# Three fused transformer blocks on one core: third mixer rescheduled, both gated merges started with the attention branch

## The chip, the cores and the metric

One NeuronCore of a Trainium2 chip runs the whole program. The metric is device time in microseconds (us) of one execution. PE is TensorE, ACT ScalarE, DVE VectorE, POOL GpSimd and SP SyncE; SP issues nearly all loads.

## What is computed

Three blocks run one after the other on x of 512 tokens by 1024 channels: a conformer/sparse attention block with MLPs, a block with an RWKV-7 branch and a sliding-window attention branch, and a block with a stick-breaking attention branch and a state-space (S5) branch. The change touches the mixers of the second and third block and the feed-forward between them:

```
# block 2, mixer                      (y_rwkv, y_att: 512 x 512)
merged = sigmoid(g_rwkv) * (y_rwkv @ w_branch_rwkv) + sigmoid(g_att) * (y_att @ w_branch_attn)
x = x + merged @ w_out
x = x + 0.5 * (silu(h @ w_gate) * (h @ w_up)) @ w_down ; x = rms_norm(x)
# block 3, mixer
q, k, v, u, g_sb, g_ssm = split(h @ w_in)
z = q k^T / 8 ; log_beta = log_sigmoid(z) ; log_one_minus = where(causal, log_beta - z, 0)
after = reverse_cumsum(log_one_minus) - log_one_minus
y_sb = (where(causal, exp(log_beta + after), 0) @ v) @ w_sb_up            # 8 heads of 64
state = powers * state + B u ; y = Re(C state) + D u                      # 32 groups, 64 states, complex
y = gelu(y) ; y = y * sigmoid(y @ w_glu + b_glu) ; y_ssm = y @ w_ssm_up
x = layer_norm(alpha * x + (1 + g_m) * ((sigmoid(g_sb) * y_sb + sigmoid(g_ssm) * y_ssm) @ w_out))
```

## The kernel before

**Split products.** Activations lie transposed (channels on partitions, 512 tokens along the free axis). Each large product is made of three TensorE passes over numbers split in a high and a low part: `hi*ah + hi*al + lo*ah` (`lin`). A weight slab of 128x2048 numbers is loaded by SP into one of three buffers `raw`, split by GpSimd into `whi` and `wlo` (lines 143 and 136, three slots each), and used by TensorE in 48 matmuls of 128x512. ACT writes the high part of an activation (`ah`, `hh`, `yh`) and DVE subtracts it for the low part (`al`, `hl`, `yl`).

**Order.** Nothing is scheduled at run time: each engine runs its own program, in the order in which the methods `*_pe`, `*_act`, `*_dve` are written, and semaphore counts say what it waits for. SP's loads follow the order in which TensorE's program asks for slabs. PSUM is a ring of six banks for `lin`; a bank is taken in program order and waits until its last reader has given it back. All small operations are recorded at helper lines (113 and 116 matmul and transpose, 131 ACT, 136 to 167 DVE).

**Second mixer.** `rwkv_order` runs the recurrence in chunks; the tiles of the recurrence lie in the memory of `whi` and `wlo`, so the first slab behind it is split only when TensorE, ACT and DVE have ended it. Then come eight high parts and eight low parts of the two branches (`yh`, `yl`), and `merge_pe`: for each half of the columns the RWKV branch, then the attention branch, 48 matmuls each. `merge_dve` multiplies the first branch's banks with gates read back from DRAM (`gr <- bank, sq`), adds the second branch, and splits the result.

**Feed-forward before the third block.** `mlp_dve` handles groups of four hidden tiles in two turns; behind each turn the call `turns(g)` lets DVE do some steps of the preparation of the state-space tables (`ssm_setup_dve`: powers L, input matrices b, angle tables T, decay rho; mostly 128x16 operations on `macc`). Behind the second turn of a group DVE must add the down-projection's eight banks to x.

**Third mixer.** `mixer3_pe` first runs eight slabs for the gates. Behind slabs 2, 4, 6 and 8 `tables_pe(j)` makes the table set j of four: 16 transposes (XT, from XB) and 16 small products (KS, from XB and WC). DVE makes XB and WC of the next set when KS of the last is done on TensorE and WC has been written to DRAM by ACT's DMA. Then come six slabs of features and two for v, and the **stick**: `stick_steps` runs 20-odd steps in which the stages of the stick-breaking attention are staggered. A stage is given a lag: step s runs `scores` of unit pair s, `sums` of s-1, `after` of s-2 and `values` of s-3. Between them, every four steps, a quarter j of the state-space branch is worked off: at step 4j+1 its inputs (`in`, bank<-U,raw), on DVE the rotation, a scan along time and the states H; at 4j+2 and 4j+3 the outputs (`y`, from U and H), and at 4j+4 the turn back. U, four shifted copies of the features u, is gathered by 16 DMAs on SP's queue (`load_u`), behind the end of the input stage. After the stick come GELU, the `glu` product and the merge as in the second block.

## Time and profile before

| | |
|---|---|
| median of 3 runs | 3972.09 us (3970.39 to 3974.9) |
| the profiled execution | 3981.96 us, its span 3980.2 us |
| TensorE busy | 3533.6 us (89%) |
| VectorE busy | 1944.2 us (49%) |
| GpSimd busy | 1623.0 us (41%) |
| ScalarE busy | 754.4 us (19%) |
| mean granted TensorE clock | 0.926 |

The profiled execution is 9.9 us (0.25%) longer than the median. A number in brackets at the end of a timeline row is how long the engine had been idle ahead of it and what ended that. Sections are found by time: the second mixer's merge is at 2399 to 2483 us, the second feed-forward at 2531 to 2932, the gates and tables of the third mixer at 2967 to 3112, the stick at 3203 to 3382, the glu product and the merge at 3393 to 3483.

### The profile page before, as it was taken

The numbers are of one execution on the slowest core, as the hardware profiler recorded it, in microseconds if no ns is written. First come the engines' busy times: TensorE is split into PE (matmuls) and PEld (weight loads), VectorE is DVE, ScalarE is ACT, GpSimd is POOL, SyncE is SP. The second block draws the span as 40 slices with busy tenths as digits, with TensorE's granted clock in tenths as the row PEclk, the third lists the DMA queues.
The fourth block names the chain that finished last, engine by engine and source line by source line (L and its number), as shares of the span: only waits on it lengthen the run. The fifth ranks groups of instructions, "written<-read, shape, count | busy, mean of one in ns | idle before, by whom it ended". The sixth has DMA issues, their size and how long they took to land. (4 is left out here: it accounts for less than half of the span.)

```text
span 3980.2 us, 44783 instructions
## 1 busy us (share of the span) xinstructions
PE 3533.6 (89%) x18996; PEld 2730.4 (69%) x18996; DVE 1944.2 (49%) x2919; ACT 754.4 (19%) x1638; POOL 1623.0 (41%) x486
## 2 busy tenths in 40 slices
PE   7989999679999999999997876999978977789998
PEld 5757888556578887788785675787746744548885
DVE  2244455337844546534245556556585235544234
ACT  2241011224521011001105221100021133121001
POOL 4404556140045666556540004565533400525552
PEclk9999999678999999999996788999989977899999
DMA  4202333220023434323420003222225232312220
GB/s 141 69 22 90 121 128 106 67 98 1 1 74 105 139 106 127 117 95 96 127 85 10 2 2 117 80 95 96 85 85 174 83 106 95 116 53 85 96 95 32
DMA packets 250679, 340.45 MB, mean 86 GB/s; under 512 B 9808, under 2 KB 180048, under 8 KB 247920
## 3 DMA queue, kind: packets, MB, share of 16 engines
q1 hardware_dynamic: 227600, 300.43, 23.1%
q10 hardware_dynamic: 22880, 37.16, 2.8%
q8 instruction: 150, 2.46, 0.2%
q14 instruction: 49, 0.40, 0.0%
HBM read 307.95 MB, written 25.43 MB: 84 GB/s over the span
## 5 line engine op out<-in xcount | busy, mean ns | idle before, releaser
L143 POOL TENSOR_SCALAR whi<-raw 128x2048 fp32r<-128x2048 f32 x241 | 487.3, 2022 | 2276.9 <-PE bank L113 1307.4
L136 POOL TENSOR_TENSOR wlo<-raw,whi 128x2048 fp32r<-128x2048 f32 x241 | 1137.2, 4718 | 20.1
L113 PE MATMUL bank<-ah,whi 128*128 128x512 f32 x2392 | 958.4, 401 | 64.3 <-DVE al L146 40.3
L113 PE MATMUL bank<-al,whi 128*128 128x512 f32 x2392 | 952.3, 398 | 0.0
L113 PE MATMUL bank<-ah,wlo 128*128 128x512 f32 x2392 | 951.0, 398 | 0.0
L113 PEld LDWEIGHTS bank<-ah,whi 128*128 128x128 f32 x2392 | 452.8, 189 | 188.2 <-issue 38.5
L113 PEld LDWEIGHTS bank<-ah,wlo 128*128 128x128 f32 x2392 | 453.1, 189 | 111.7
L113 PEld LDWEIGHTS bank<-al,whi 128*128 128x128 f32 x2392 | 453.2, 189 | 110.4 <-issue 1.2
L113 PE MATMUL bank<-hh,whi 128*128 128x512 f32 x1040 | 414.2, 398 | 14.5 <-DVE x L146 14.5
L113 PE MATMUL bank<-hl,whi 128*128 128x512 f32 x1040 | 412.9, 397 | 0.0
L113 PE MATMUL bank<-hh,wlo 128*128 128x512 f32 x1040 | 412.9, 397 | 0.0
L113 PEld LDWEIGHTS bank<-hh,whi 128*128 128x128 f32 x1040 | 196.5, 189 | 63.5 <-DVE x L146 15.8
L113 PEld LDWEIGHTS bank<-hh,wlo 128*128 128x128 f32 x1040 | 196.2, 189 | 48.2
L113 PEld LDWEIGHTS bank<-hl,whi 128*128 128x128 f32 x1040 | 196.5, 189 | 47.7
L136 DVE TENSOR_TENSOR scr<-gt,bank 128x512 f32<-128x512 f32 x66 | 45.2, 686 | 343.8 <-PE bank L113 343.2
L136 DVE TENSOR_TENSOR hl<-scr,hh 128x512 fp32r<-128x512 f32 x66 | 200.3, 3072 | 0.2
L136 DVE TENSOR_TENSOR x<-x,bank 128x512 f32<-128x512 f32 x128 | 86.0, 685 | 162.1 <-PE bank L113 162.1
L146 DVE SCALAR_TENSOR_TENSOR x<-bank,x 128x512 f32<-128x512 f32 x120 | 80.0, 687 | 165.8 <-PE bank L113 165.8
L131 ACT ACTIVATE gt<-gt 128x512 f32<-128x512 f32 x108 | 68.2, 634 | 394.1 <-DVE gt L136 391.2
L131 ACT ACTIVATE hh<-gt 128x512 fp32r<-128x512 f32 x64 | 40.0, 625 | 535.9 <-DVE gt L146 535.9
L136 DVE TENSOR_TENSOR hl<-gt,hh 128x512 fp32r<-128x512 f32 x64 | 126.5, 1998 | 28.0 <-ACT gt L131 28.0
L146 DVE SCALAR_TENSOR_TENSOR gt<-bank,rb 128x512 f32<-128x512 f32 x64 | 44.1, 691 | 147.5 <-PE bank L113 147.3
(388 smaller groups left out, 4320.9 us busy)
## 6 DMA issues: line engine op xcount, KB each, us to landing
raw<-in_w_in SPq DMA_DIRECT2D x34, 1024.0 KB, 5.3
raw<-in_w_mlp_in SPq DMA_DIRECT2D x32, 1024.0 KB, 5.5
raw<-in_w_mlp_out SPq DMA_DIRECT2D x32, 1024.0 KB, 6.6
raw<-in_w_ada SPq DMA_DIRECT2D x24, 1024.0 KB, 5.2
raw<-in_ffn_w_gate SPq DMA_DIRECT2D x22, 1024.0 KB, 5.3
raw<-in_ffn_w_up SPq DMA_DIRECT2D x22, 1024.0 KB, 5.3
raw<-in_ffn_w_down SPq DMA_DIRECT2D x22, 1024.0 KB, 5.0
raw<-in_w_ffn_in SPq DMA_DIRECT2D x22, 1024.0 KB, 5.0
```

The lines of the kernel that those rows point to most:

```text
L113: return self.eng.matmul(out, lhsT, rhs, start=start, stop=stop, skip_group_check=True)
L131: return self.eng.activation(out, src, func, scale=scale, **kw)
L136: return IDLE if self.eng is None else self.eng.tensor_tensor(out, a, b, op)
L143: return self.eng.tensor_scalar(out, a, s1, s2, op0, op1)
L146: return IDLE if self.eng is None else self.eng.scalar_tensor_tensor(out, a, s, b, op0, op1)
```

## The change

Five things, in the order of the program. (1) Both merges begin with the attention branch; its high and low parts are made during the recurrence (in the second mixer beside `scan(2)`, in the third in steps 16 to 18 of the stick). (2) `ssm_setup_dve` is cut at the input matrices: 8 steps a turn in place of 20 (and 15 in place of 18 in the first part), and the angle tables (`ssm_turns_dve`) are made behind the last table set. (3) `tables_pe` is divided: XT stays where it was, KS comes one slab later. (4) The first gather of U goes into the tile yM, which is not lent from the weight buffers, and no longer waits for the end of the input stage. `values` runs at lag 4, the scan and H one step after the rotation, y at lags 3 and 4, the turn at lag 6. (5) In the third mixer the first merge block stands ahead of glu. Its slab may be split when the last `after` product and the third quarter's outputs are done, and glu's slab when `lw` of the last unit and the last quarter's outputs are done.

```diff
+    def ended(self, name):
+
+        return lambda: [x.at("end", name) for x in (self.P, self.C, self.D)]
...
-                    self.some(first, 18)
+                    self.some(first, 15)
                 elif g > 2:
-                    self.some(second, 20)
+                    self.some(second, 8)
...
-        self.merge_pe(e, "mrg2", self.mrg2, (A["w_branch_rwkv_2"][0], A["w_branch_attn_2"][0]), "rwkv")
+        self.merge_pe(e, "mrg2", self.mrg2, (A["w_branch_rwkv_2"][0], A["w_branch_attn_2"][0]),
+                      lambda i: self.ended("rwkv"))
...
+    def high_of_branch_act(self, a, name, T, br, src, tiles=range(4)):
+        for k in tiles:
+            a.f(T["hi"][br][:, k, :], src[:, k, :], ACT.Copy).then_inc(*self.C.up(name, "hi part", br, k))
+
+    def low_of_branch_dve(self, d, name, T, br, src, tiles=range(4)):
+        for k in tiles:
+            d.wait_ge(*self.C.at(name, "hi part", br, k))
+            d.tt(T["lo"][br][:, k, :], src[:, k, :], T["hi"][br][:, k, :].bitcast(F), SUB).then_inc(
+                *self.D.up(name, "lo part", br, k))
+
+    @staticmethod
+    def merge_order(T):
+
+        return [(half, br) for half in range(2) for br in (T["first"], 1 - T["first"])]
+
+    def merge_pe(self, e, name, T, Ws, after, between=None):
+
+        for i, (half, br) in enumerate(self.merge_order(T)):
+            self.lin(e, (name, half, br), Ws[br], 0, 4, [512 * half + 128 * n for n in range(4)],
+                     lambda k, br=br: (T["hi"][br][:, k, :], T["lo"][br][:, k, :]),
+                     lambda k, br=br: self.D.at(name, "lo part", br, k), after=after(i))
+            if i == 0 and between:
+                between()
...
+        self.U4 = [t["yM"], far["U1"], far["U0"], far["U1"]]
...
-                 between=lambda n: self.tables_pe(e, n // 4) if n % 4 == 2 else None)
+        def tables(n):
+            if n % 4 == 2:
+                self.tables_in_pe(e, n // 4)
+            elif n:
+                self.tables_own_pe(e, n // 4 - 1)
+        self.lin(e, "gates3", W, 0, 8, [2048 + 128 * n for n in range(16)], self.xact, normed, between=tables)
         self.lin(e, "feat", W, 0, 8, [128 * n for n in range(8)] + [1536 + 128 * n for n in range(4)], self.xact,
-                 normed)
+                 normed, between=lambda n: None if n else self.tables_own_pe(e, 3))
...
+        assert Clock.draft or self.n_split % 3 == self.MERGE_SLOT, self.n_split
+        first = lambda: [P.at("st", "a", 31), P.at("ssm", 2, "y", 1)]
+        second = lambda: [D.at("st", "lw", 31), P.at("ssm", 3, "y", 1)]
+
+        def glu():
+            self.lin(e, "glu", A["w_glu_3"][0], 0, 4, [128 * n for n in range(4)],
+                     lambda k: (self.ah[:, 4 + k, :], self.al[:, 4 + k, :]), lambda k: D.at("glu", "lo", k), after=second)
+        self.merge_pe(e, "mrg3", self.mrg3, (A["w_sb_up_3"][0], A["w_ssm_up_3"][0]),
+                      lambda i: self.ended("stick") if i else first, glu)
...
+        def tables(n):
+            if n and n % 4 == 0:
+                self.tables_in_act(a, n // 4 - 1)
+            elif n > 4 and n % 4 == 2:
+                self.tables_own_act(a, n // 4 - 1)
+        self.gates_act(a, "gates3", self.gates3, tables)
+        self.tables_in_act(a, 3)
+        self.tables_own_act(a, 3)
...
+        d.wait_ge(*C.at("nmix3", "hi", 7))
+        self.ssm_turns_dve(d)
...
-        self.stick_steps((3, values), (2, after), (0, scores), (None, lambda s: self.ssm_pe(e, s)))
+        self.stick_steps((4, values), (2, after), (0, scores), (None, lambda s: self.ssm_pe(e, s)))
...
+        def early(s):
+
+            if 16 <= s < 19:
+                a.wait_ge(*P.at("st", "s", 31))
+                a.wait_ge(*C.now())
+                self.high_of_branch_act(a, "mrg3", self.mrg3, 0, m["yS"], [s - 16])
+        self.stick_steps((None, lambda s: self.ssm_act(a, s)), (4, values), (2, after), (0, scores), (None, early))
...
-        self.stick_steps((3, values), (2, after), (1, sums), (None, lambda s: self.ssm_dve(d, s)))
+        def early(s):
+            if 16 <= s < 19:
+                self.low_of_branch_dve(d, "mrg3", self.mrg3, 0, self.m3["yS"], [s - 16])
+        self.stick_steps((3, values), (2, after), (1, sums), (None, lambda s: self.ssm_dve(d, s)), (None, early))
...
+    def ssm_turns_dve(self, d):
+
+        D, m, tmp = self.D, self.m3, self.scr.tiles[2]
+        T, rho, t16 = [m["T0"], m["T1"]], m["rho"], tmp[:, 0:16]
+        co, si, m8, er, ei, e2r, e2i = (self.small[:, i, :] for i in (4, 5, 7, 12, 13, 14, 15))
+        d.wait_ge(*D.now())
+        self.cmul_dve(d, (er, ei), (co, si), (co, si), t16)
+        d.wait_ge(*D.now())
+        run(self.turns_of_angles(d, T, rho, tmp, t16, m8, er, ei, e2r, e2i))
...
-        e.wait_ge(*self.P.at("end", "mix3 in"))
-        if j > 1:
-            e.wait_ge(*self.P.at("ssm", j - 2, "y", 1))
+        if j:
+            e.wait_ge(*self.P.at("end", "mix3 in"))
+        else:
+            e.wait_ge(*self.P.at("tables", 3, "KS", 1))
+            e.wait_ge(*self.tab_out["WC"].at(3))
+        if j == 3:
+            e.wait_ge(*self.P.at("ssm", 1, "y", 1))
...
-        j = self.ssm_piece(s, 4)
+        j = self.ssm_piece(s, 6)
...
-            j = self.ssm_piece(s, 2 + q2)
+            j = self.ssm_piece(s, 3 + q2)
...
+        j = self.ssm_piece(s, 2)
+        if j is not None:
+            js = slice(4 * j, 4 * j + 4)
+            rh = m["rho"][:, js, :].rearrange("p q m -> p (q m)")
+            last()
+            d.scan(hr, rh, gr, 0.0, MUL, ADD).then_inc(*D.up())
+            d.scan(hi, rh, gi, 0.0, MUL, ADD).then_inc(*D.up())
+            last()
+            if j:
...
+    def other_branch(self):
+
+        self.a.wait_ge(*self.D.at("wkv", 1, "ARBK"))
+        for k in range(4):
+            yield
+            self.net.high_of_branch_act(self.a, "mrg2", self.net.mrg2, 1, self.net.m2["yA"], [k])
```

TensorE at the first table set, before: the last two transposes of XB, KS (WC with XB), and the next gate slab (ah, al with whi). "waits" names the engines whose semaphores are awaited.

```order
L116 MATMUL bank<-cst,XB_186_115 128x128
L116 MATMUL bank<-cst,XB_187_116 128x128
L113 MATMUL bank<-WC_188_117,XB_186_115 32x256 [waits dve,act]
L113 MATMUL bank<-WC_189_118,XB_187_116 32x256
...
L113 MATMUL bank<-WC_188_117,XB_186_115 32x256
L113 MATMUL bank<-WC_189_118,XB_187_116 32x256
L113 MATMUL bank<-ah,whi_6 128x512 [waits pool,act]
L113 MATMUL bank<-al,whi_6 128x512
```

The same KS products after the change: they stand behind the slab in whi_6, and ahead of that in whi_4.

```order
L113 MATMUL bank<-al,whi_6 128x512
L113 MATMUL bank<-ah,wlo_9 128x512
L113 MATMUL bank<-WC_190_119,XB_188_117 32x256 [waits dve,act]
L113 MATMUL bank<-WC_191_120,XB_189_118 32x256
...
L113 MATMUL bank<-WC_190_119,XB_188_117 32x256
L113 MATMUL bank<-WC_191_120,XB_189_118 32x256
L113 MATMUL bank<-ah,whi_4 128x512 [waits pool,act]
L113 MATMUL bank<-al,whi_4 128x512
```

48 matmuls have come between the transposes and KS.

SP at the end of the third mixer's input loads, as a piece of the difference: the 16 DMAs of the first gather (U or yM from u).

```order
 L106 DMA raw_2<-in_w_in 128x4x512 [waits pool]
-L106 DMA U_222_151<-u_102 32x512 [waits tab_WC,act,tab_TM,pe,tab_XT,pool]
-L106 DMA U_222_151<-u_102 32x512 x3
-L106 DMA U_222_151<-u_102 32x511 x4
-L106 DMA U_222_151<-u_102 32x510 x4
-L106 DMA U_222_151<-u_102 32x509 x4
+L106 DMA yM_105<-u_104 32x512 [waits tab_WC,act,tab_TM,pe,tab_XT,pool]
+L106 DMA yM_105<-u_104 32x512 x3
+L106 DMA yM_105<-u_104 32x511 x4
+L106 DMA yM_105<-u_104 32x510 x4
+L106 DMA yM_105<-u_104 32x509 x4
 L106 DMA raw_3<-tables 128x2048
```

The place in the queue is the same; the destination is another, and the count of TensorE's semaphore behind "pe" is now that of the last KS product.

VectorE in the first quarter of the stick, before: scan (scr from rho), the products that give the states H, and then the logarithms `lw` of the step behind.

```order
L167 SCALAR_TENSOR_TENSOR scr_18<-rho_113,scr_17 128x256 [waits dve]
L167 SCALAR_TENSOR_TENSOR scr_18<-rho_113,scr_17 128x256
L136 TENSOR_TENSOR H_224_153<-scr_18,T_182_111 128x4x64 [waits dve]
L136 TENSOR_TENSOR rb<-scr_18,T_183_112 128x256
L136 TENSOR_TENSOR H_224_153<-H_224_153,rb 128x4x64 [waits dve]
L136 TENSOR_TENSOR H_225_154<-scr_18,T_183_112 128x4x64
L136 TENSOR_TENSOR rb<-scr_18,T_182_111 128x256 [waits dve]
L136 TENSOR_TENSOR H_225_154<-H_225_154,rb 128x4x64 [waits dve]
L136 TENSOR_TENSOR lw_214_143<-lw_214_143,bank 128x128 [waits pe,dve]
L136 TENSOR_TENSOR lw_215_144<-lw_215_144,bank 128x128 [waits pe]
```

After: rotation, then the step's logarithms, and only a step later scan and H.

```order
L136 TENSOR_TENSOR rb<-bank,T_185_114 128x256 [waits dve]
L136 TENSOR_TENSOR scr_17<-scr_17,rb 128x256 [waits dve]
L136 TENSOR_TENSOR lw_208_137<-lw_208_137,bank 128x128 [waits pe]
...
L167 SCALAR_TENSOR_TENSOR scr_18<-rho_115,scr_17 128x256 [waits dve]
L167 SCALAR_TENSOR_TENSOR scr_18<-rho_115,scr_17 128x256
L136 TENSOR_TENSOR H_226_155<-scr_18,T_184_113 128x4x64 [waits dve]
L136 TENSOR_TENSOR rb<-scr_18,T_185_114 128x256
L136 TENSOR_TENSOR H_226_155<-H_226_155,rb 128x4x64 [waits dve]
L136 TENSOR_TENSOR H_227_156<-scr_18,T_185_114 128x4x64
L136 TENSOR_TENSOR rb<-scr_18,T_184_113 128x256 [waits dve]
L136 TENSOR_TENSOR H_227_156<-H_227_156,rb 128x4x64 [waits dve]
```

Between the rotation and the scan 12 instructions of the attention now stand (the first is shown, 11 are left out at the dots).

## Rows read from the trace of the kernel before

**Rows 1.** The page, costliest groups: busy us, mean ns | idle before, releaser.
```profile
L113 PE MATMUL bank<-ah,whi 128*128 128x512 f32 x2392 | 958.4, 401 | 64.3 <-DVE al L146 40.3
```

**Rows 2.** Waits of PE, whole span: total us, times, longest us.
```profile
PE bank L113 <- DVE lw L136: 38.6, 8, 7.0
...
PE bank L113 <- DVE WC L136: 23.6, 4, 9.5
...
PE bank L113 <- DMA raw<-tables: 13.9, 1, 13.9
...
PE bank L113 <- DVE H L136: 3.9, 1, 3.9
```

**Rows 3.** Timeline, second mixer's merge: start us, us, instruction [idle before <-releaser].
```profile
2401.41 14.14 DVE L136 TENSOR_TENSOR yl<-yR,yh 128x512 fp32r<-128x512 f32 x4 [0.76 <-ACT yh L131]
...
2407.76 0.79 PE L113 MATMUL bank<-yh,whi 128*128 128x512 f32 x1 [8.55 <-POOL wlo L136]
...
2431.36 0.77 PE L113 MATMUL bank<-yh,whi 128*128 128x512 f32 x1 [10.17 <-DVE gr L136]
```

**Rows 4.** Timeline, second feed-forward: VectorE and TensorE.
```profile
2656.60 1.39 DVE L136 TENSOR_TENSOR gt<-bank,rb 128x512 f32<-128x512 f32 x2 [9.81 <-PE bank L113]
...
2723.80 1.39 DVE L136 TENSOR_TENSOR gt<-bank,rb 128x512 f32<-128x512 f32 x2 [9.81 <-PE bank L113]
...
2771.64 4.68 DVE L136 TENSOR_TENSOR b<-b,tmp 128x256 f32<-128x256 f32 x1
...
2798.05 1.39 DVE L136 TENSOR_TENSOR gt<-bank,rb 128x512 f32<-128x512 f32 x2 [9.81 <-PE bank L113]
...
2873.26 1.39 DVE L136 TENSOR_TENSOR gt<-bank,rb 128x512 f32<-128x512 f32 x2 [9.81 <-PE bank L113]
...
2905.87 0.51 PE L113 MATMUL bank<-hh,whi 128*128 128x512 f32 x1 [3.94 <-DVE x L146]
```

**Rows 5.** Timeline, third mixer's gates and tables.
```profile
2995.10 3.61 PE L113 MATMUL bank<-WC,XB 128*32 128x256 f32 x16 [1.41 <-DVE WC L136]
...
3032.53 5.68 PE L113 MATMUL bank<-WC,XB 128*32 128x256 f32 x16 [9.47 <-DVE WC L136]
...
3038.62 1.56 ACTq L106 DMA_DIRECT2D tables<-WC  x2
...
3045.56 1.29 DVE L136 TENSOR_TENSOR g<-L,b 128x512 f32<-128x512 f32 x2 [13.18 <-DMA tables<-WC]
...
3052.69 5.72 DVE L136 TENSOR_TENSOR g<-L,sp 128x576 f32<-128x576 f32 x2
```

**Rows 6.** Windows: PE, PEld, DVE, ACT, POOL busy, PEclk; one period of the stick.
```profile
3298.00:3338.70 40.70, 29.82 (x133) 18.16 (x133) 22.13 (x65) 14.84 (x35) 0.00 (x0) 0.79 0.32 103
```

**Rows 7.** TensorE by shape in 3298.0 to 3338.7: busy us, mean ns | idle.
```profile
L113 PE MATMUL bank<-U,raw 128*128 128x64 f32 x33 | 4.4, 302 | 0.0
L113 PE MATMUL bank<-raw,U 128*64 128x256 f32 x16 | 4.3, 393 | 0.0
L113 PE MATMUL bank<-raw,H 128*64 128x256 f32 x16 | 4.1, 379 | 0.0
L113 PE MATMUL bank<-mb,cst 128*128 128x512 f32 x4 | 3.8, 1047 | 0.0
```

**Rows 8.** Timeline, the stick: TensorE and VectorE.
```profile
3255.20 1.02 PE L113 MATMUL bank<-mb,cst 128*128 128x512 f32 x2
...
3301.90 0.42 DVE L136 TENSOR_TENSOR scr<-bank,T 128x256 f32<-128x256 f32 x1 [2.43 <-PE bank L113]
...
3308.86 1.97 PE L113 MATMUL bank<-lw,v 128*64 128x512 f32 x4 [7.00 <-DVE lw L136]
```

**Rows 9.** Timeline, after the stick: GpSimd and TensorE.
```profile
3388.23 4.81 POOL L136 TENSOR_TENSOR wlo<-raw,whi 128x2048 fp32r<-128x2048 f32 x1
...
3393.14 0.77 PE L113 MATMUL bank<-yh,whi 128*128 128x512 f32 x1 [11.18 <-POOL wlo L136]
...
3421.25 0.77 PE L113 MATMUL bank<-yh,whi 128*128 128x512 f32 x1 [14.22 <-DVE yl L136]
```

More of the change, by code:

```diff
@@ L330, in gpsimd @@
             raw, hi, lo = self.raw[slot], self.whi[j % self.NSPL], self.wlo[j % self.NSPL]
-            if after:
-                for other in (self.P, self.C, self.D):
-                    g.wait_ge(*other.at("end", after))
+            for w in after() if after else ():
+                g.wait_ge(*w)
             g.wait_ge(*self.raw_in[slot].at(i))
@@ L1899, in merge_act @@
         for i, (half, br, n) in enumerate(order):
+            if i == 4 and between:
+                between()
             if i + 1 < 16:
                 bring(i + 1)
-            if br:
+            if br != T["first"]:
                 m = 4 * half + n
@@ new lines, in merge_dve @@
+        for half, br in self.merge_order(T):
+            if i == 4 and between:
+                between()
+            for n in range(4):
+                m, key, second = 4 * half + n, ((name, half, br), n), br != T["first"]
+                g = self.sq.of(name, half, br, n)
+                if second:
+                    s, free = self.scr.take(name, m)
+                    d.wait_ge(*free)
+                d.wait_ge(*self.P.at(*key))
+                d.wait_ge(*self.gate_in[i % 2].at(name, half, br, n))
+                i += 1
+                dst = s[:, :] if second else T["gr"][:, n, :]
+                d.tt(dst, self.ps.of(*key)[:, :], g[:, :], MUL).then_inc(*self.ps.give(D, *key))
+                self.sq.also(D, name, half, br, n)
+                if second:
+                    d.wait_ge(*D.now())
+                    d.tt(s[:, :], s[:, :], T["gr"][:, n, :], ADD).then_inc(*D.up(name, "value", m))
+                    d.wait_ge(*self.C.at(name, "hi", m))
+                    d.tt(self.al[:, m, :], s[:, :], self.ah[:, m, :].bitcast(F), SUB).then_inc(
+                        *self.scr.give(D, name, m))
@@ L1940, in rwkv_order @@
         run(together(e.inverse(1, 0), e.inverse(1, 1), e.parts(1)))
-        run(e.scan(2))
+        run(together(e.scan(2), e.other_branch()))
         run(together(e.scan(3), e.post(2)))
@@ L2076, in mixer3_pe @@
         self.barrier(e, P, "stick", True)
-        T = self.mrg3
-        self.lin(e, "glu", A["w_glu_3"][0], 0, 4, [128 * n for n in range(4)],
-                 lambda k: (T["yh"][:, k, :], T["yl"][:, k, :]), lambda k: D.at("glu", "yl", k), after="stick")
-        self.merge_pe(e, "mrg3", T, (A["w_sb_up_3"][0], A["w_ssm_up_3"][0]))
+        assert Clock.draft or self.n_split % 3 == self.MERGE_SLOT, self.n_split
[6 more added lines that the diff above has]
+                      lambda i: self.ended("stick") if i else first, glu)
         self.lin(e, "out3", A["w_out_3"][0], 0, 8, [128 * n for n in range(8)], self.xact,
@@ L2502, in tables_act, with tables_own_act @@
                 ACT.Copy).then_inc(*self.ps.give(C, "tables", j, "XT", q))
+        a.wait_ge(*C.at("tables", j, "XT", 3))
+        a.dma(self.tables[j, 0], t["XT"][:, :, :, :, :].rearrange("p q b r n -> p (q b r n)")).then_inc(
+            *out["XT"].up(j))
+    def tables_own_act(self, a, j):
+        P, C, D, t, out = self.P, self.C, self.D, self.tab_t, self.tab_out
         if j:
@@ L2511, in tables_act @@
                 *self.ps.give(C, "tables", j, "KS", q2))
-        a.wait_ge(*C.at("tables", j, "XT", 3))
-        a.dma(self.tables[j, 0], t["XT"][:, :, :, :, :].rearrange("p q b r n -> p (q b r n)")).then_inc(
-            *out["XT"].up(j))
         for ri in range(2):
@@ new lines, in ssm_dve @@
+        j = self.ssm_piece(s, 2)
+        if j is not None:
+            js = slice(4 * j, 4 * j + 4)
+            rh = m["rho"][:, js, :].rearrange("p q m -> p (q m)")
+            last()
+            d.scan(hr, rh, gr, 0.0, MUL, ADD).then_inc(*D.up())
+            d.scan(hi, rh, gi, 0.0, MUL, ADD).then_inc(*D.up())
+            last()
+            if j:
+                d.wait_ge(*P.at("ssm", j - 1, "y", 1))
+            q3 = lambda ap: ap.rearrange("p (q m) -> p q m", q=4)
+            self.cmul_dve(d, [x[:, :, 1:65] for x in self.H], [q3(hr), q3(hi)], [x[:, js, :] for x in T], q3(w))
+            D.mark("ssm", j, "H")
@@ L3232, in post, with other_branch @@
         d.tt(m["yR"][:, :, at], m["yR"][:, :, at], t4, ADD).then_inc(*net.scr.give(D, "wkv", "t", p))
+    def other_branch(self):
+        for k in range(4):
+            yield
+            self.net.low_of_branch_dve(self.d, "mrg2", self.net.mrg2, 1, self.net.m2["yA"], [k])
 def _constants():
```

195 lines of the change are left out of this document (74 added, 121 removed).

## Prediction

> **What bounds the kernel now.** I read the page's busy shares first: TensorE 89%, VectorE 49%, GpSimd 41%. Nine tenths of TensorE's time are products with a weight slab [rows 1], which the change leaves as they are: 48 matmuls, 11.2 us a slab (a feed-forward group of six slabs takes 67.20 us, below). So time can only come from TensorE's waits and from its slow stretches. Second, the list of its waits over the span [rows 2]: `lw` of VectorE 38.6 us in 8 waits, `WC` 23.6 in 4, a table load 13.9 in one, `H` 3.9 in one. All four lie in the third mixer. Third, the timelines around them and around the two merges [rows 3, 5, 8, 9], and the second feed-forward [rows 4], where a wait shows at one place only although three groups are stretched. Last the window table of one period of the stick [rows 6]: in 40.70 us TensorE is busy 29.82 and its granted clock is 0.79. Neither engine fills the period; they wait for each other in turn.
>
> All sums are made against the profiled execution, 3981.96 us, 9.9 above the median.
>
> **Second mixer's merge: -11 us.** The first wait, 8.55 us, is for GpSimd's split of a slab that may begin only behind the recurrence [rows 3]; the change leaves that condition, so it stays. The second is 10.17 us for the gate product `gr` [rows 3]. It is late because VectorE first makes eight `yl`, four in 14.14 us, so 3.5 each. The attention's four now move beside the recurrence. The other four end at 2401.4 + 14.1 = 2415.5. The first branch's four banks come from one slab, side by side, at about 2407.8 + 11.2 + 1 = 2420, and are multiplied then; TensorE, which ran out of banks at 2431.4 - 10.2 = 2421.2, waits under 1: -9.5. Behind the wait the first matmul takes 0.77 us where the mean is 401 ns [rows 1, 3]; without the pause this slow restart goes: -2. The moved instructions are four copies and four `yl`; they land in a place where VectorE is short, and cost 0 to 3 us, I take 0.7 (free of GpSimd a 128x512 product of VectorE takes 1.39 / 2 = 0.7 [rows 4]). Range 7 to 12.5.
>
> On the 3.5 us: in the timeline a `yl` takes five times as long while GpSimd splits [rows 3]. The Trainium skill ("SBUF — State Buffer", Who interferes with whom) says that a VectorE instruction with two SBUF inputs and a GpSimd one that reads SBUF exclude each other for whole instructions; by that rule, the trace agrees.
>
> **Second feed-forward: -19 us.** The multiplication `gt` marks the same point in each group, always after an idle of 9.81 us [rows 4]. From 2656.60 to 2723.80 a group takes 67.20 us, which is the bare six slabs; the next two take 74.25 and 75.21. They lose 7.05 and 8.01, and a third one at the end has its wait in the list, 3.94 [rows 4], with about 1.5 of slow restart. Together 20.6. The cause is the 20 table steps a turn: VectorE comes late to the bank additions. One 128x256 step caught by a GpSimd split takes 4.68 [rows 4]. With 8 steps a turn the additions start in time, unless such a step is caught again; for that I take off 1.5. The angle tables that were made here go behind the last table set, where TensorE has eight slabs of features and v (8 x 11.2 = 90 us) that ask nothing of them. They are some 90 instructions, most on 128x16; even at 0.7 each that is 63: 0, and if GpSimd stretches them past the 90, the stick starts late by the excess. Range 12 to 21.
>
> **Gates and tables: -11 us.** Now TensorE waits for `WC` at every KS (one 9.47 [rows 5]), 23.6 in all, and three of the four KS run slow, 5.68 where the first takes 3.61 [rows 5]: 3 x 2.1 and some 1.3 on the slabs behind, 7.6. With one slab (11.2) between XT and KS both go: -31. But VectorE may begin the next XB only when KS of the last set is done and `WC` is stored. That chain now starts 11.2 us later and only one slab is left ahead of the next XT. From the DMA's issue to VectorE's restart the trace has 3038.62 to 3045.56, 7 us; XB itself takes 3045.56 to 3052.69, 7.1 [rows 5], and 4 us more when GpSimd catches it. 14.1 to 18.4 against 11.2: XT waits 3 to 7, once more than that since the first `WC` store was slower; I take 5, three times, 15, and 5 for slow restarts. -31 + 20 = -11. Range 2 to 18.
>
> **The stick: -54 us.** It lasts 179 us now (3203 to 3382). What goes: the table load 13.9, which queues on SP behind 16 gather DMAs that wait for the end of the input stage; `H` 3.9; `lw` 38.6, since a quarter's rotation, scan and H now stand in two steps. 56.4 in all [rows 2]. One of these `lw` waits is 7.00, and VectorE's run of the quarter begins at 3301.90, 6.3 us before its first logarithm [rows 8].
> What comes: `y` now waits for H, which VectorE makes one step behind the rotation. VectorE's way from `in` to H is 6.3 (the quarter's own work) + 0.75 (yM) + the attention's share of a step, (22.1 - 7.05)/4 = 3.8 [rows 6]: 10.9. TensorE has two steps of attention between, (29.8 - 3.5 - 12.8)/4 = 3.4 each, where 3.5 is slow clock (next sentence) and 12.8 the state-space products [rows 6, 7], + 0.7: 7.5. So 3.4 a period, about 13 over four. The clock: four `mb` products take 3.8 us, 1047 ns each [rows 7], two take 1.02 at the upper level [rows 8]; that is 1.8 lost on them, I estimate as much on their neighbours, 3.5 a period, 14 in all. With shorter waits I count 11 of it back. -56.4 + 13 - 11 = -54. A period becomes about 29 us; its floor is TensorE's 26.3 (29.8 - 3.5), above VectorE's 22.1 [rows 6]. The gather into yM has its 16 DMAs earlier in SP's queue behind the same loads; the three later gathers have whole periods. Range 40 to 60.
>
> **After the stick: -8.5 us.** Now TensorE waits 11.18 for a slab whose split can begin only when all is done (`wlo` alone 4.81) and 14.22 for `yl` [rows 9]. The first merge block's slab is split some 3 us before the stick ends: the split takes between 4.81 and 11.18 us, I take 6.7, and the wait becomes about 3.5. Behind that block, glu needs four low parts of GELU at 3.5 each under GpSimd's lock, 14, against its 11.2 us: a new wait of about 4.4. The 14.22 falls to about 9, as its first branch's parts are done and `gr` is needed later, but `yl` of the second still follows glu. 7.7 - 4.4 + 5.2 = 8.5. Range 2 to 14. The split meets VectorE's last `lw` steps; one caught instruction there costs up to 4.8.
>
> **Sum.** -11 - 19 - 11 - 54 - 8.5 = -103.5: 3878.5 in a profile like the one shown, 3869 on the median's level.
>
> **Rivals.**
> *A, the tables' wait only moves.* XT comes late by what KS was late: with the chain at 18.4 twice and at 22 once the waits are 7.2, 7.2 and 11, 11 more than the 15 taken. For it: VectorE idles 13.18 for the store [rows 5], so the chain, not VectorE, is the limit. Against: two of three XB runs are short. The gates gain 0: 3880.
> *B, the stick becomes bound by VectorE's latency.* Each of its instructions for a step waits for TensorE and the reverse, and 22.1 busy us come with idle before each. The period stays 35: 4 x 6 more than forecast, 3893. For it: VectorE waits 2.43 for a bank even at the rotation [rows 8]. Against: the two-step distance gives each side a spare step.
> *C, the gather isn't earlier.* It stands at the same place on SP's queue, behind waits for slabs; if the slab loads ahead set its time, the 13.9 stay: 3883.
> *D, slower: TensorE stays at its lower clock through the stick.* The rows show both levels there: 1047 ns and 510 ns for the same `mb` product, which is 1.2 against 2.4 GHz [rows 7, 8]. If the denser row of small products with short waits were granted the lower level throughout, its 26.3 a period double to 52.6, 4 x 52.6 + 10 = 220 against 179 now: +41, less the 50 gained elsewhere. It decides once this reaches the slabs: a merge block at the lower level costs 11.2 more, so from one block on the kernel is slower, and with all five of merge and glu +47, 4019. Against: waits shrink, and in the page's row all slabs average 401 ns, the upper level.
> [...]
>
> **How the numbers follow.** Forecast 0.66, A 0.12, B 0.15, C 0.03, D 0.04. The likeliest gives 3869; its own terms, taken apart, reach from 3850 to 3890, and B to 3893; with gaps added up the range is 3850 to 3905. A measurement of this kernel tells 0.2% (8 us) from no change. Every case but D lies 60 us or more below; of D half is within 0.2% and half slower: faster 0.96, same 0.02, slower 0.02.
>
> **What would show it.** Merge 2: no wait by `gr` over 2 us, the 8.5 before it still there. Feed-forward: all `gt` distances 67.2. Gates: no wait by `WC`, KS at 3.6, three waits by XB of 3 to 10. Stick: no wait by the table load, `lw` under 5 in all, waits by `H` about 13, period near 29, clock above 0.9. Tail: TensorE back within 4 us, a wait by `al` of about 4 before glu. Wrong if the stick's period stays above 33, if the clock there falls, or if the angle tables delay the first step.

## The result

| | before | changed |
|---|---|---|
| median | 3972.77 us (3970.39 to 3974.9, 4 runs) | 3847.99 us (3846.75 to 3848.68, 4 runs) |
| ratio | | 0.9686, 95% interval 0.9669 to 0.9703 |
| profiled execution, span | 3980.2 us | 3846.9 us |
| TensorE busy, mean granted clock | 3533.6 us, 0.926 | 3495.2 us, 0.942 |

124.8 us faster (3.1%). The forecast was 3869 us with a range of 3850 to 3905: the direction and four fifths of the size are right, and the time is 2 us below the range. The two profiles differ by 133.3 us, more than the medians, since the profiled execution before was a long one. By stretches that is as follows. A stretch goes from the first product of one part on TensorE to the first product of the next; only the stick is counted to the end of its last product, where the row of glu and the merge begins.

| stretch, us | before | changed | difference | forecast |
|---|---|---|---|---|
| up to the second mixer's merge | 2407.8 | 2402.2 | -5.6 | 0 |
| second merge, up to the feed-forward | 123.6 | 109.2 | -14.4 | -11 |
| second feed-forward | 401.6 | 380.5 | -21.1 | -19 |
| norms between | 34.2 | 34.2 | 0 | 0 |
| gates, tables, features, v | 235.7 | 205.4 | -30.3 | -11 |
| stick | 179.1 | 129.2 | -49.9 | -54 |
| glu and third merge | 101.1 | 87.5 | -13.6 | -8.5 |
| rest | 497.1 | 498.8 | +1.7 | 0 |

The first row can't be put down to the change. The changed kernel and its eleven variants below, alike up to that point, reach the merge between 2394.2 and 2407.5 us, and the kernel before reached it at 2407.8 and, in the last experiment, at 2400.5. Most of this comes from one stretch of the recurrence and from what lies ahead of it; the last section has the numbers. A few microseconds between the medians of two kernels say little here; a later stretch that an edit leaves alone repeats within 1 or 2 us (2.5 for the second merge). So the experiments are read by stretches first.

### The profile page after: what moved, and what is told of

Its sections match the earlier page's. It is cut to its first block, busy times and chain, and to the rows that moved or that the text cites. A ratio compares the mean times of both kernels' runs of the same rounds, so it can differ in the third digit from the quotient of the medians.

```text
span 3846.9 us, 44799 instructions
## 1 busy us (share of the span) xinstructions
PE 3495.2 (91%) x18996; PEld 2710.7 (70%) x18996; DVE 1898.0 (49%) x2919; ACT 751.9 (20%) x1638; POOL 1620.0 (42%) x486
## 4 chain that ended last, share of the span: by engine, by line
PE 84%; DVE 10%; ACT 3%; issue 1%; DMA 1%; POOL 1%; ACTq 0%; DVEq 0%; SPq 0%; POOLq 0%
PE bank L113 81%; PE bank L116 3%; DVE scr L136 1%; DVE al L146 1%; DVE rb L136 1%; DVE rb L158 1%; DVE x L146 1%; DVE st L151 0%; ACT ah L131 0%; ACT L131 0%; DMA raw<-in_ffn_w_gate 0%; POOL wlo L136 0%; ACTq L106 0%; ACT p L131 0%; DMA macc<-in_masks 0%
## 5 line engine op out<-in xcount | busy, mean ns | idle before, releaser
L146 DVE SCALAR_TENSOR_TENSOR gt<-bank,rb 128x512 f32<-128x512 f32 x64 | 44.1, 691 | 146.7 <-PE bank L113 146.5
```

Source lines behind the costliest of these rows:

```text
L146: return IDLE if self.eng is None else self.eng.scalar_tensor_tensor(out, a, s, b, op0, op1)
```

## The profile after

TensorE's waits in the changed kernel (us in total, times, longest). In [rows 2] stood `lw` 38.6, `WC` 23.6, table load 13.9, `H` 3.9.

```profile
PE bank L113 <- DVE lv L136: 8.7, 4, 7.9
...
PE bank L113 <- DVE yl L136: 8.1, 1, 8.1
...
PE bank L113 <- DVE gr L136: 5.4, 2, 2.7
...
PE bank L113 <- DVE H L136: 4.9, 3, 2.2
...
PE bank L113 <- ACT yM L131: 4.9, 1, 4.9
```

`WC` and the table load are gone, and no `XB` has come. For `lw` (half of it is called `lv` now) TensorE waits once for long, at the stick's end. One wait is new and stood in no forecast: `rs` of VectorE, 8.0 us in four waits of the stick, the longest 3.8.

```profile
PE bank L113 <- DVE rs L155: 8.0, 4, 3.8
```

Timeline of the second merge and of `gt` in the feed-forward:

```profile
2402.15 0.79 PE L113 MATMUL bank<-yh,whi 128*128 128x512 f32 x1 [8.54 <-POOL wlo L136]
...
2427.76 0.47 PE L113 MATMUL bank<-yh,whi 128*128 128x512 f32 x1 [1.60 <-DVE scr L136]
```

```profile
2636.36 1.39 DVE L136 TENSOR_TENSOR gt<-bank,rb 128x512 f32<-128x512 f32 x2 [9.81 <-PE bank L113]
...
2703.56 1.39 DVE L136 TENSOR_TENSOR gt<-bank,rb 128x512 f32<-128x512 f32 x2 [9.81 <-PE bank L113]
...
2770.76 1.39 DVE L136 TENSOR_TENSOR gt<-bank,rb 128x512 f32<-128x512 f32 x2 [9.81 <-PE bank L113]
...
2837.96 1.39 DVE L136 TENSOR_TENSOR gt<-bank,rb 128x512 f32<-128x512 f32 x2 [9.81 <-PE bank L113]
```

The wait of 10.17 [rows 3] is gone, the 8.5 ahead of it has stayed, and all three distances of `gt` are 67.20, where two were longer [rows 4]. Both steps did what the prediction wrote, with one exception: a second, shorter wait by `gr` stands in the merge, 2.72 us in the kernel before and 2.72 now, and the prediction had said that none over 2 us would be left.

The tables, by engine (TensorE, ScalarE's queue, VectorE, GpSimd); these answer to [rows 5]:

```profile
2950.71 1.91 PE L116 MATMUL bank<-cst,XB 128*128 128x128 f32 x16
2963.75 3.64 PE L113 MATMUL bank<-WC,XB 128*32 128x256 f32 x16
2978.62 1.91 PE L116 MATMUL bank<-cst,XB 128*128 128x128 f32 x16
```

```profile
2954.39 0.33 ACTq L106 DMA_DIRECT2D tables<-XT  x1
...
2967.43 0.94 ACTq L106 DMA_DIRECT2D tables<-WC  x2
```

```profile
2972.24 1.29 DVE L136 TENSOR_TENSOR g<-L,b 128x512 f32<-128x512 f32 x2 [18.35 <-DMA tables<-WC]
...
2976.34 1.40 DVE L136 TENSOR_TENSOR XB<-g,g 64x512 f32<-64x512 f32 x2
```

```profile
2965.96 4.58 POOL L136 TENSOR_TENSOR wlo<-raw,whi 128x2048 fp32r<-128x2048 f32 x1
2978.94 2.04 POOL L143 TENSOR_SCALAR whi<-raw 128x2048 fp32r<-128x2048 f32 x1 [8.40 <-PE bank L113]
```

KS ends at 2967.4. The store of `WC` releases VectorE at 2972.24, 4.8 us later, and XB is done at 2977.74, after 5.5 us. XT could not start before 2978.62, the end of its slab. XB lies exactly in the gap between GpSimd's two splits (it ends at 2970.54 and begins again at 2978.94). The chain from the end of KS to the end of XB is 10.4 us against the slab's 11.2, so there is no wait, with 0.9 us to spare.

One period of the stick in the changed kernel (the columns of [rows 6]), and a wait of TensorE in it:

```profile
3174.50:3203.50 29.00, 25.11 (x132) 16.55 (x133) 21.93 (x66) 14.19 (x35) 0.00 (x0) 1.00 0.45 146
3203.50:3234.05 30.55, 26.76 (x132) 17.04 (x133) 21.88 (x66) 14.29 (x35) 0.00 (x0) 0.94 0.39 141
```

```profile
3203.51 1.74 PE L113 MATMUL bank<-raw,U 128*64 128x256 f32 x4 [2.16 <-DVE H L136]
```

29.0 and 30.6 us where there were 40.7, at a clock of 1.00 and 0.94 where it was 0.79. TensorE's busy time for what are nearly the same products (132 and 133 in the rows) fell from 29.8 to 25.1 and 26.8, with the higher clock in the same rows.

The end of the stick, VectorE, TensorE and GpSimd:

```profile
3251.40 5.04 DVE L136 TENSOR_TENSOR yl<-yS,yh 128x512 fp32r<-128x512 f32 x1 [1.36 <-ACT yh L131]
3256.36 2.17 DVE L136 TENSOR_TENSOR lv<-lv,cst 128x128 f32<-128x128 f32 x2
```

```profile
3258.68 1.98 PE L113 MATMUL bank<-lv,v 128*64 128x512 f32 x4 [7.93 <-DVE lv L136]
3265.51 0.80 PE L113 MATMUL bank<-yh,whi 128*128 128x512 f32 x1 [4.85 <-ACT yM L131]
```

```profile
3251.39 4.50 POOL L136 TENSOR_TENSOR wlo<-raw,whi 128x2048 fp32r<-128x2048 f32 x1
```

GpSimd's early `wlo` (the last row) and a `yl` that now stands ahead of the last masks begin together; the `yl` takes 5.04 in place of 0.69, the masks come some 5 us late, and the last product waits for them. With the `rs` above, these are the new waits of size that the change made.

## The experiments

All are the changed kernel with one edit undone or added, except the last, which is the kernel before with one edit; a row that starts with "and" adds its edit to the row above. Ratio is to the kernel before, measured again beside each group (medians 3975.1 to 3977.8 us), with its 95% interval; the other columns are stretches in us (gates is the stretch from the first gate product to the stick).

| run | median, us | ratio | feed-forward | gates | stick | glu, merge |
|---|---|---|---|---|---|---|
| changed kernel | 3848.0 | 0.9686 (0.9669 to 0.9703) | 380.5 | 205.4 | 129.2 | 87.5 |
| KS undivided | 3862.4 | 0.9712 (0.9690 to 0.9734) | 380.5 | 225.4 | 129.8 | 87.3 |
| XB 2.7 us later | 3879.2 | 0.9756 (0.9738 to 0.9774) | 380.4 | 235.3 | 129.9 | 87.5 |
| XT's store late | 3886.5 | 0.9775 (0.9761 to 0.9790) | 380.5 | 241.4 | 130.2 | 87.9 |
| both table edits undone | 3883.6 | 0.9766 (0.9752 to 0.9781) | 381.1 | 233.6 | 129.8 | 88.8 |
| setup as before | 3870.9 | 0.9732 (0.9712 to 0.9752) | 401.1 | 204.3 | 130.0 | 87.6 |
| old lags | 3889.9 | 0.9785 (0.9763 to 0.9807) | 380.5 | 204.8 | 170.8 | 87.1 |
| late gather | 3869.6 | 0.9733 (0.9719 to 0.9748) | 381.6 | 204.8 | 146.7 | 87.4 |
| no early split | 3848.6 | 0.9685 (0.9669 to 0.9701) | 380.5 | 204.8 | 122.9 | 94.2 |
| masks ahead of yl | 3844.2 | 0.9670 (0.9656 to 0.9684) | 380.5 | 205.2 | 121.3 | 88.2 |
| and GELU behind the mark | 3846.1 | 0.9675 (0.9661 to 0.9688) | 380.5 | 205.0 | 122.0 | 91.3 |
| and a later third split | 3836.5 | 0.9648 (0.9635 to 0.9662) | 380.5 | 205.0 | 122.0 | 84.2 |
| before, XT's store early | 3960.8 | 0.9962 (0.9949 to 0.9976) | 401.6 | 217.9 | 179.8 | 101.1 |

### The gates, where the forecast missed

**KS undivided.**

```diff
             if n % 4 == 2:
                 self.tables_in_pe(e, n // 4)
-            elif n:
-                self.tables_own_pe(e, n // 4 - 1)
+                self.tables_own_pe(e, n // 4)
```

> The changed kernel with KS put back directly behind the transposes; all else stays. Theory: the division alone is worth the whole 30.4 us that the stretch from the first gate product to the stick's first product became shorter, so 3848 + 30 = 3878, with four waits for WC of 1 to 10 us in the trace. Rival, the forecast's own price: the division is worth 11 us and the other 19 come from how the splits happen to fall elsewhere; then 3859.

The stretch grew by 20.0 us, not by 30 and not by 11. A third of the gain was not the division's. In the four sets KS waited 1.4, 7.6, 0 and 6.1, where [rows 2] had 23.6 in all. The median, 3862.4, lies near the rival's 3859, but this execution reached the second merge 8 us early, so the stretch decides. Neither number expected was right, and 10 us were without a cause.

**XB 2.7 us later.**

```diff
             d.wait_ge(*self.tab_out["WC"].at(j - 1))
+            l0, b0 = ...
+            for i in range(4):
+                d.tt(t[f"g{i % 2}"][:, :, 0:8, :], l0, b0, MUL).then_inc(*self.D.up())
+                d.wait_ge(*self.D.now())
```

> The changed kernel with four extra 128x512 products of VectorE (some 2.7 us) ahead of XB in three of the four table sets. Theory: XT waits for nothing only because the store (4.85) and XB (5.5) make 10.4 us, under the slab's 11.2, and because XB fits between two splits of GpSimd; pushed 2.7 later it passes the slab by 1.9 and its last operations meet the next split, so XT waits 2 to 7 us three times: 3854 to 3872 with the slow restarts. Rival: XB has room to spare, so that the forecast's chain was wrong in kind and not in size; then no wait and 3848.

VectorE and TensorE in this run:

```profile
2982.59 1.29 DVE L136 TENSOR_TENSOR g<-L,b 128x512 f32<-128x512 f32 x2
2983.92 7.16 DVE L136 TENSOR_TENSOR XB<-g,g 64x512 f32<-64x512 f32 x2
```

```profile
2991.23 3.64 PE L116 MATMUL bank<-cst,XB 128*128 128x128 f32 x16 [7.75 <-DVE XB L136]
```

Three times 2.7 us of VectorE's cost 29.9 us of the stretch (three waits of 7.75 to 7.94, most of the rest slow restarts: the transposes take 3.64 in place of 1.91). The last pair of XB takes 7.16 in place of 1.40: GpSimd's split begins at 2983.64, within it. The theory holds in kind and its price was too low: waits of 2 to 7 and at most 3872 us were expected, and the run took 3879.2. The room of 0.9 us is real, and 2.7 us more of work cost 10 us a set.

**XT's store late.** The diff has a second edit that the prediction did not price: when `tables_act` was cut in two, the store of XT went with the first half, so it is issued 13 us ahead of the stores of WC (2954.39 and 2967.43) and no longer directly ahead of them (3038.26 and 3038.62 before).

```diff
-        a.wait_ge(*C.at("tables", j, "XT", 3))      # in tables_in_act
-        a.dma(self.tables[j, 0], t["XT"]...)
...
+        a.wait_ge(*C.at("tables", j, "XT", 3))      # in tables_own_act, ahead of the stores of WC
+        a.dma(self.tables[j, 0], t["XT"]...)
```

> The changed kernel with one order of stores put back: the store of XT (one DMA) again behind the evacuation of KS, just ahead of the stores of WC, as before; the division stays. Theory: the changed kernel also moved this store away, and that is why the wait for the WC store fell from 7 us to 4.85; with it back the chain is some 12.5 us against a slab of 11.2, XB meets the next split, and XT waits 5 to 8 us three times, so that the stretch from gates to stick goes from 205 us to 225 to 235 (3868 to 3878). Rival: the division alone took the waits away and the store is a detail: stretch within 3 us of 205, time within 5 of 3848.

```profile
2968.31 1.54 ACTq L106 DMA_DIRECT2D tables<-WC  x2
```

```profile
2976.66 1.29 DVE L136 TENSOR_TENSOR g<-L,b 128x512 f32<-128x512 f32 x2 [22.21 <-DMA tables<-WC]
...
2982.45 5.58 DVE L136 TENSOR_TENSOR XB<-g,g 64x512 f32<-64x512 f32 x2
```

```profile
2988.18 3.65 PE L116 MATMUL bank<-cst,XB 128*128 128x128 f32 x16 [8.88 <-DVE XB L136]
3026.82 3.61 PE L116 MATMUL bank<-cst,XB 128*128 128x128 f32 x16 [8.38 <-DVE XB L136]
...
3065.67 3.65 PE L116 MATMUL bank<-cst,XB 128*128 128x128 f32 x16 [9.10 <-DVE XB L136]
```

With XT's store directly ahead, the store of WC takes 8.35 us from its issue to VectorE's restart (2968.31 to 2976.66; 8.0 and 8.6 in the other two sets) and 4.81 without it (2967.43 to 2972.24; 4.8 in all three sets). XT's transposes then wait 26.4 us in all. The stretch is 241.4, longer than before the change. The theory's direction held; it had expected 225 to 235.

**Both table edits undone.** The two edits above together.

> The changed kernel with both table edits undone: KS directly behind the transposes and the store of XT behind KS. Theory: KS alone put back gave a stretch of 225.4 us, 10.3 short of the 235.7 of before; the store's place is those 10.3, so the stretch is 234 to 237 and the time some 3878. Rival: the 10.3 come from something else that changed around (the preparation, the angle tables), then the stretch stays near 225 and the time near 3862 to 3868.

233.6, against 235.7 in the kernel before: the theory is right within 0.4. So the four combinations of the two edits are:

| gates, us | XT's store late | XT's store early |
|---|---|---|
| KS directly behind XT | 233.6 | 225.4 |
| KS one slab later | 241.4 | 205.4 |

The division without the store costs 7.8 us; with it, it gains 20.0. The store is worth 8.2 alone and 36.0 with the division. One reason lies in the order of ScalarE's program: with KS directly behind XT, the store of XT can't be issued 13 us ahead of those of WC in every set. In the run with KS undivided it stood 3.3, 12.8 and 2.1 us ahead, and VectorE restarted 8.3, 4.8 and 6.7 us after the stores of WC were issued.

**Before, XT's store early.** The three lines of the store moved up in `tables_act` of the kernel before, nothing else.

> The kernel before with one line moved: the store of XT is issued ahead of the evacuation of KS in place of behind it; KS stays directly behind the transposes. Theory: the store is worth 8 to 10 us by itself (with KS undivided the stretch was 233.6 with it late and 225.4 with it early), so the stretch from gates to stick becomes 225 to 228 and the time 3962 to 3965. Rival: it only pays with the division; then the stretch stays at 235 and the time at 3972.

The stretch went from 235.7 to 217.9, the time to 0.9962 of before: some 15 us for one moved store. The stretch is 7 to 10 us shorter than the theory's 225 to 228. The run with KS undivided has 225.4 with the same order of TensorE's products in the gates; the 7.5 us between the two are mainly the fourth set, where KS waited 1.38 here and 6.06 there, with a slower restart behind it. Whether a split catches XB or WC moves one set by 5 us, and nothing here controls it. So the 8.2 of the table and the 17.8 here bound what the store is worth without the division.

### The setup and the stick

**Setup as before.** 18 and 20 steps a turn, and the angle tables behind them.

```diff
-                    self.some(first, 15)
+                    self.some(first, 18)
-                    self.some(second, 8)
+                    self.some(second, 20)
```

> The changed kernel with 18 and 20 preparation steps a turn and the angle tables back in the second feed-forward. Theory: the three late groups return, +21: 3869, with waits of TensorE by x of 4 to 6 us. Rival: the angle tables behind the table sets cost something themselves (the first step of the stick, or the splits they hold up), and moving them back returns part of it: 3855 to 3862.

The feed-forward returned to 401.1 (+20.6), with waits by `x` of 4.74, 5.83 and 3.94, as the theory had it, and the gates got 1.1 shorter. The moved angle tables cost 1 us at most; the rival is refuted.

**Old lags.** `values` at 3, scan and H in the rotation's step, y at 2 and 3, the turn at 4.

```diff
-        self.stick_steps((4, values), (2, after), ...
+        self.stick_steps((3, values), (2, after), ...
-        j = self.ssm_piece(s, 2)        # scan and H
+        j = self.ssm_piece(s, 1)
```

> The changed kernel with the lags of the stick as before (values 3, scan and H in the rotation's step, y at 2 and 3, turn at 4); the early gather stays. Theory: the stick was 179.1 us with a 13.9 us wait for the gather; without that wait and with the old lags it is 165 against 129 now: +36, 3884, period back at 40 us and the granted clock near 0.79 in it. Rival: most of the 50 us came with the gather, whose early data let all later steps start in time; then under +20, below 3868.

The stick took 170.8, +41.6, with waits for `lv` of 46.7 us; the period (3216.03 to 3256.84) was 40.8 us at a clock of 0.79, as before the change. The lags carry most of the stick's gain. The theory had expected 165. The difference is the last wait, which the other edits of the changed kernel made. The kernel before and this run:

```profile
3380.88 1.08 PE L113 MATMUL bank<-lw,v 128*64 128x512 f32 x4 [1.86 <-DVE lw L136]
```

```profile
3295.84 1.98 PE L113 MATMUL bank<-lv,v 128*64 128x512 f32 x4 [9.36 <-DVE lv L136]
```

As in the changed kernel, a `yl` of 5.03 us at 3288.56 stands beside GpSimd's early `wlo` and ahead of the last masks; the run without the early split, below, shows what that costs.

**Late gather.**

```diff
-        if j:
-            e.wait_ge(*self.P.at("end", "mix3 in"))
-        else:
-            e.wait_ge(*self.P.at("tables", 3, "KS", 1))
-            e.wait_ge(*self.tab_out["WC"].at(3))
+        e.wait_ge(*self.P.at("end", "mix3 in"))
```

> The changed kernel in which the first gather of U again waits for the end of the input stage. Theory, from the run with the old lags (stick 170.8 us against 179.1 before): the early gather is worth 8 to 9 us and not the 13.9 of the wait it removes, since part of that wait hid VectorE's and ScalarE's first steps: stick 129 becomes 137 to 138, time 3856. Rival, the forecast's price: +13.9 us, 3862.

```profile
3151.04 7.06 PE L113 MATMUL bank<-yM,raw 128*128 128x64 f32 x32 [13.74 <-DMA raw<-tables]
```

146.7, +17.5, which neither had expected. Here the wait stands in full (13.74), and the products behind it run slowly (7.06 where the changed kernel has 4.04). The theory's 8 to 9 us came from 179.1 - 170.8 = 8.3, the gather's worth with the old lags. But the 170.8 held 7.5 us of the last wait just shown. Counted from the stick's first product to the start of its last wait, the four combinations are:

| stick without its last wait, us | late gather | early gather |
|---|---|---|
| old lags | 176.1 | 159.5 |
| new lags | 136.8 | 119.3 |

The gather is worth 16.6 with the old lags and 17.5 with the new ones, the lags 39.3 and 40.2. So these two edits add up within 1 us.

### The end of the stick

**No early split.** The slabs of the first merge block and of glu are split behind the stick's end.

```diff
-                      lambda i: self.ended("stick") if i else first, glu)
+                      lambda i: self.ended("stick"), glu)
```

> The changed kernel in which the slabs of the first merge block and of glu are split only when the stick has ended on all engines, as before; the order of the products stays. Theory: in the changed kernel the early split (it begins at 3249.4) catches VectorE's yl (5.04 and 4.33 us in place of 0.69) and with it the last masks, so the last product waits 7.93 us; without it that wait falls to about 1.5 and the 4.85 behind it becomes the split itself, about 7 to 11. The early split is then worth under 4 us: 3846 to 3852. Rival, the forecast's price: the early split is worth 7.7 us, 3856.

```profile
3252.73 1.08 PE L113 MATMUL bank<-lv,v 128*64 128x512 f32 x4 [1.89 <-DVE lv L136]
3266.19 0.77 PE L113 MATMUL bank<-yh,whi 128*128 128x512 f32 x1 [12.38 <-POOL wlo L136]
```

The stick ends 6.3 us earlier, and the merge begins 1.2 us later (135.3 us behind the stick's start, 134.0 in the changed kernel): 217.1 against 216.7 for both stretches together. The early split gains nothing. What the stretch behind the stick gained, 101.1 to 94.2 without it, is left for the new order of the products and the attention's early parts; no run undoes those alone.

**Masks ahead of yl.**

```diff
-            if 16 <= s < 19:
-                self.low_of_branch_dve(d, "mrg3", self.mrg3, 0, self.m3["yS"], [s - 16])
+            if s == 16:
+                self.low_of_branch_dve(d, "mrg3", self.mrg3, 0, self.m3["yS"], [0, 1])
```

> The changed kernel with one order of VectorE's put right: the high and low parts of tiles 0 and 1 are both made in step 16, tiles 2 and 3 behind the stick, so that no yl stands between the last logarithms and the last masks. Theory: the last masks run before GpSimd's wlo begins, the wait of 7.93 us falls to 1.5 to 2.5, the 4.85 (GELU) stays: 6 us less, 3842. Rival: GpSimd's split catches the masks themselves instead of the yl, as the two begin within a microsecond; then 3847 or more.

The 7.93 became 1.04, both stretches together 209.5, 7.2 less, as the theory had it (6). The medians alone (3844.2 against 3848.0) would not tell this.

**GELU behind the mark.** ScalarE marks the end of the stick ahead of its four GELU, not behind them.

> As the run with the masks ahead of yl, and GELU stands behind ScalarE's end-of-stick mark, so that TensorE doesn't wait for it before the first merge block. Theory: the 4.85 us falls to what wlo of the first slab leaves, 1 to 3: another 2 to 4 us, 3839. Rival: glu's low parts come later than before and a wait ahead of glu takes its place: no gain over the run before.

The wait fell only to 3.29, and behind the block a wait of 4.66 for `gr` took its place: GpSimd now splits four slabs in a row (3251.66 to 3280.1), and glu's four low parts take 14.69 us on VectorE:

```profile
3261.03 14.69 DVE L136 TENSOR_TENSOR al<-yM,ah 128x512 fp32r<-128x512 f32 x4
```

Both stretches are 213.3, 3.8 more than without it; the rival was right.

**A later third split.**

```diff
-                      lambda i: self.ended("stick") if i else first, glu)
+                      lambda i: [first, self.ended("stick"), lambda: [D.at("mrg3", "lo part", 1, 3)],
+                                 self.ended("stick")][i], glu)
```

> As the run with GELU behind the mark, and the slab of the third merge block is split only when the last yl of the state-space branch is made. Theory: the 8.10 us wait by yl is VectorE under GpSimd's wlo (four yl in 6.79, the products before them 4.39); without the split beside them TensorE restarts within 2 to 3 us: 5 to 6 us less, 3833. Rival: the later split makes the block behind it wait as long: no gain over 3839.

```profile
3287.64 0.47 PE L113 MATMUL bank<-yh,whi 128*128 128x512 f32 x1 [2.20 <-DVE yl L136]
3304.25 0.76 PE L113 MATMUL bank<-yh,whi 128*128 128x512 f32 x1 [5.17 <-DVE scr L136]
```

The 8.10 became 2.20, a later wait grew from 1.60 to 5.17, and both stretches are 206.2, 7.1 below the run before and 10.5 below the changed kernel. This is the fastest version: 3836.53 us (3830.45 to 3839.31, 5 runs), 0.9648 of before. Its interval lies below that of the changed kernel (0.9635 to 0.9662 against 0.9669 to 0.9703), by little.

## Why the prediction came out as it did

The profiles differ by 29.8 us more than the 103.5 forecast. 19.3 of that is the gates, 5.6 the first row of the table, which no step of the change explains, and the rest small terms both ways.

**Second merge: right in mechanism, a little small.** -14.4 for -11, outside the range by 2. 10.2 of it is the wait by `gr`. The slower products behind that pause had cost 3.0 and a second slow restart 1.2 more, where the prediction had taken 2. The copies and `yl` moved into the recurrence cost little: from `sA` (last section) to the merge the kernel before took 231.4 and 231.7 us in two profiles, the changed one and its variants 232.7 to 233.1 in ten of twelve, so about 1.4 for the 0.7 taken.

**Feed-forward: right.** -21.1 for -19. No 128x256 step was caught, so the 1.5 taken off for that was not needed.

**Gates: the step that failed, "From the DMA's issue to VectorE's restart the trace has 3038.62 to 3045.56, 7 us; XB itself takes ... 7.1, and 4 us more when GpSimd catches it."** The first half of the sum, -31 for KS's waits and slow runs, came out (-30.3). The second half, +20, was to come from a chain longer than the slab. Its form was right, and both durations in it were wrong for the changed kernel. The 7 us held only while XT's store stood directly ahead on the queue: it is 4.8 without and 8.0 to 8.6 with (the run with the store late). The prediction did not list that the store moved. The 7.1 held a split that caught XB; in the changed kernel XB begins 4.8 us behind KS, falls between two splits and takes 5.5. So 10.4 against 11.2, not 14.1 to 18.4, and the 20 us priced for waits and restarts were 0. Rival A describes what happens with the store late: three waits of 8.4 to 9.1, though the stretch of 241.4 is longer than A's, which gained nothing.

**Stick: right in mechanism, -49.9 for -54, in part by luck.** The period is 29.0 to 30.6 for 29, the clock 0.94 to 1.00. The waits fell from 56.4 to 21.6: `lv` 8.7, `H` 4.9 and `rs` 8.0. For `H` 13 was forecast, and `rs` was not foreseen; that the two make 12.9 together is luck. The last wait, for `lv`, is 7.93 where 1.86 stood before; the prediction spoke of it only as a risk of 4.8. It gave some 7 us back: without it the stick gained 56.8. What is left for the clock is 15.1 (49.9 less the waits' 34.8) for 11; it is a remainder, which no run measured by itself. That the gather and the lags add up was right.

**After the stick: sum too small, -13.6 for -8.5.** The first wait fell from 11.18 to 4.85, and the second from 14.22 to 8.10, about as forecast (7.7 and 5.2). The wait before glu, +4.4 in the sum, did not come (its own terms, 14 against 11.2, give only 2.8): the four low parts took 8.61 us, not 14. And the early split's 7.7 is worth 0.4 once what it costs the stick's end is counted. Taking the order and the split as one step hid that one gains and the other does not.

**Rivals B, C and D** did not occur: the period is near 29, the gather came early, and the clock rose.

The low end of the range, 3850, was missed by 2 us. The terms' own upper ends (12.5, 21, 18, 60 and 14) would have reached 3847. The one far off was the gates' 18: in every case considered there the waits of KS were replaced by new ones.

## To carry to other kernels

When a step is cut in two, list which DMAs go with which half before pricing a chain through the same queue; a landing time read from a trace belongs to the queue as it stood, and here it changed by 3.5 us and turned a loss of 8 us into a gain of 20. Where a chain fits beside a slab, write both lengths and where GpSimd's splits fall: 10.4 against 11.2 was free, 13.1 against 11.2 cost 10 us a set. Price edits in one stretch as the four combinations of a table: the store gave 8.2 us alone and 36.0 with the division. Where two edits don't seem to add up, look first whether a third one changes the end of the stretch: the stick's two edits seemed to miss 9 us, and that was one wait counted twice.

## What the runs showed of the hardware

- GpSimd's split makes a VectorE instruction with two inputs in SBUF wait even where both begin within 0.01 us: `yl` 5.04 us at 3251.40, beside `wlo` from 3251.39 to 3255.89. Four such against splits in a row took 14.69 us in the run with GELU behind the mark. The Trainium skill ("SBUF — State Buffer", Who interferes with whom) has the rule, that whoever issues first holds the shared ports for its whole instruction; by that rule, the trace agrees.
- Two stores (WC, 512 KB each) issued 0.36 us behind a store of XT (1 MB) on the same queue released VectorE 8.35 us after their issue. In the changed kernel, with the store of XT 13 us ahead, it was 4.81 us.
- The granted clock of 312 matmuls of the recurrence was 0.65 in one execution and 0.74 in another, and the window below is 5.8 us longer. Windows of the kernel before and of the changed one (columns as in [rows 6]):

```profile
2106.00:2176.00 70.00, 56.08 (x312) 37.31 (x312) 41.96 (x169) 38.04 (x133) 0.00 (x0) 0.65 0.04 14
```

```profile
2104.87:2169.03 64.16, 49.68 (x312) 33.05 (x313) 41.77 (x169) 38.19 (x133) 0.00 (x0) 0.74 0.05 15
```

The change is not the cause. From the first transposes `at` to the first product of `sA` the kernel before took 70.3 us at 0.65 here and 64.1 us at 0.74 in the run with the store early, with the same program up to there. Over all 14 profiles this stretch took 64.0 to 64.5 us at 0.74 to 0.76 (seven), 68.5 at 0.70 (one), 70.2 to 70.4 at 0.65 (five) and 74.1 at 0.59 (one). It began between 2097.1 and 2106.0 us, and from its end to the second merge the changed kernel and its variants took 231.1 to 235.7 us, ten of the twelve 232.7 to 233.1. These three parts make up the 13.3 us (2394.2 to 2407.5) by which the merge's start differed. Why the clock differed stays open.
